# Turning norm rows and memory probabilities: eight 128x128 transposes a tile, or 32 products on the quarters of the array

## What is computed

```python
def rmsnorm(x, g):
    xf = x.astype(F32)
    y = xf * lax.rsqrt(jnp.mean(xf * xf, axis=-1, keepdims=True) + EPS)
    return (y * g.astype(F32)).astype(x.dtype)

# hybrid_layer, behind the mixer (gated DeltaNet, short conv, stick-breaking attention)
x = x + jnp.concatenate([y_a, y_b, y_c], axis=-1) @ w_mix_out

h = rmsnorm(x, norm_mem_g)                                        # "norm2" in the kernel
qm = rmsnorm((h @ w_mq).reshape(B, T, MEM_HEADS, MEM_DH), mq_norm_g)
s = jnp.einsum('bthd,bnhd->bhtn', qm, mem_k) * (MEM_DH ** -0.5)
p = jax.nn.softmax(s, axis=-1)                                    # 4 heads, 256 memory tokens
om = jnp.einsum('bhtn,bnhd->bthd', p, mem_v).reshape(B, T, MEM_W)
x = x + om @ w_mo

h = rmsnorm(x, norm_ffn_g)                                        # "norm3" in the kernel
gt, ffn_buf_new = causal_dwconv(h @ w_gate, ffn_buf, ffn_conv_w)
x = x + (jax.nn.silu(gt) * (h @ w_up)) @ w_down
```

## Time and profile before

| | |
|---|---|
| median of 3 runs | 947.84 us |
| profiled execution, time | 947.93 us |
| profiled execution, span | 946.2 us |
| TensorE busy | 934.1 us, 99% |
| DVE busy | 648.3 us, 69% |
| ACT busy | 451.9 us, 48% |
| POOL busy | 170.1 us, 18% |

### The profile page before, as it was taken

How to read it: one execution, slowest core, us unless ns; L and a number is a source line. 1 busy time by engine, 2 the same in 40 slices (tenths; PEclk the granted TensorE clock), 3 DMA queues, 4 the chain that set the end, 5 groups by cost and what they waited for, 6 DMA issues and landing times.

```text
span 946.2 us, 16664 instructions
## 1 busy us (share of the span) xinstructions
PE 934.1 (99%) x6807; PEld 847.1 (90%) x6807; DVE 648.3 (69%) x1083; ACT 451.9 (48%) x836; POOL 170.1 (18%) x198
## 2 busy tenths in 40 slices
PE   8999999999999999999999999999999999999998
PEld 7899888998889877899889999999999999888886
DVE  7627888777775556551666999999999999435321
ACT  6634444648565344464655445444444446333310
POOL 0071101103654331000002042222222220000000
PEclk9999999999999999999999999999999999999999
DMA  8624152121104084143903322222222224312221
GB/s 302 225 87 145 56 169 90 48 94 46 45 5 134 2 278 166 61 150 150 317 35 116 132 90 90 89 90 90 76 74 77 87 89 147 152 59 97 76 91 55
DMA packets 73819, 103.69 MB, mean 110 GB/s; under 512 B 2576, under 2 KB 53904, under 8 KB 73360
## 3 DMA queue, kind: packets, MB, share of 16 engines
q1 hardware_dynamic: 73744, 102.63, 32.0%
HBM read 92.27 MB, written 10.35 MB: 108 GB/s over the span
## 4 chain that ended last, share of the span: by engine, by line
PE 90%; DVE 4%; ACT 2%; issue 1%; POOL 1%; DMA 1%; SPq 0%; ACTq 0%; DVEq 0%; POOLq 0%
PE bank L1202 8%; PE bank L1204 8%; PE bank L1203 8%; PE bank L533 7%; PE bank L535 7%; PE bank L534 7%; PE bank L495 6%; PE bank L497 5%; PE bank L496 5%; PE bank L463 3%; PE bank L559 2%; PE bank L561 2%; PE bank L560 2%; PE bank L482 1%; PE bank L481 1%; PE bank L483 1%
## 5 line engine op out<-in xcount | busy, mean ns | idle before, releaser
L2150 DVE TENSOR_TENSOR wlo<-wraw,whi 128x2048 fp32r<-128x2048 f32 (+1 forms) x56 | 126.1, 2253 | 103.1 <-ACT whi L1599 93.8
L1599 ACT ACTIVATE whi<-wraw 128x2048 fp32r<-128x2048 f32 (+1 forms) x58 | 109.3, 1885 | 102.7 <-PE bank L535 72.9
L495 PE MATMUL bank<-hhi,whi 128*128 128x320 f32 x352 | 116.4, 331 | 0.6 <-issue 0.6
L497 PE MATMUL bank<-hhi,wlo 128*128 128x320 f32 x352 | 108.7, 309 | 0.0
L496 PE MATMUL bank<-hlo,whi 128*128 128x320 f32 x352 | 108.7, 309 | 0.0
L495 PEld LDWEIGHTS bank<-hhi,whi 128*128 128x128 f32 x352 | 66.2, 188 | 5.0 <-issue 3.6
L496 PEld LDWEIGHTS bank<-hlo,whi 128*128 128x128 f32 x352 | 66.2, 188 | 3.0 <-issue 2.4
L497 PEld LDWEIGHTS bank<-hhi,wlo 128*128 128x128 f32 x352 | 66.1, 188 | 0.0
L533 PE MATMUL bank<-whi,hhi 128*128 128x512 f32 x150 | 58.4, 389 | 0.0
L534 PE MATMUL bank<-wlo,hhi 128*128 128x512 f32 x150 | 58.4, 389 | 0.0
L535 PE MATMUL bank<-whi,hlo 128*128 128x512 f32 x150 | 58.3, 389 | 0.0
(11 more groups left out here) (489 smaller groups left out, 2701.9 us busy)
## 6 DMA issues: line engine op xcount, KB each, us to landing
wraw<-in_w_in SPq DMA_DIRECT2D x13, 1024.0 KB, 5.3
wraw<-in_w_gate SPq DMA_DIRECT2D x11, 1024.0 KB, 5.1
wraw<-in_w_up SPq DMA_DIRECT2D x11, 1024.0 KB, 5.1
wraw<-in_w_down SPq DMA_DIRECT2D x10, 1024.0 KB, 5.0
kTs<-in_cache_sb_k SPq DMA_DIRECT2D x8, 512.0 KB, 4.4
vraw<-in_cache_sb_v SPq DMA_DIRECT2D x8, 512.0 KB, 5.0
wraw<-in_w_mix_out SPq DMA_DIRECT2D x4, 1024.0 KB, 6.1
kmT<-in_cache_mem_k SPq DMA_DIRECT2D x8, 512.0 KB, 6.0
```

The lines of the kernel that those rows point to most:

```text
L495: T.matmul(o, wh[:, k, cs], hhi[:, k, hs], start=(k == 0), stop=False)
L497: ins = T.matmul(o, wl[:, k, cs], hhi[:, k, hs], start=False, stop=(k == KD - 1))
L1599: V(wv(whi, i), wv(wraw, i), ACT.Copy).then_inc(s["w_hi_ready"], 1)
L2150: V.tensor_tensor(wv(wlo, i), wv(wraw, i), wv(whi, i).bitcast(F32), ALU.subtract)\
```

## The change

`turn_rows` and, for the prompt's four tiles, `mem_probs` call a new helper, `turn_quarters`. For each 128x128 block of the source it issues four products of 64x64: row half g of the block (64 tokens) and column half c (64 features) is the stationary operand, the matching quarter of the unit matrix is the moving one. The product with g and c writes partitions of half c, in the bank of g. So a bank now holds all eight blocks for one half of the tile's tokens, where it held four blocks for all of its tokens. Both banks are taken ahead of the first product and both are marked full behind the last ones. The readers follow: hi_part and lo_part, and the copies of probT, take 8 pieces of 64 tokens instead of 4 of 128. The queries' first half of the tokens now asks for tiles 0, 1 and one half of tile 2. The samples' probabilities are turned as before, by eight 128x128 transposes.

```diff
--- before.py
+++ after.py
@@ -279,6 +279,9 @@
         def quad(b):
             return bank[b][:, :].rearrange("p (a b) -> p a b", a=4)
 
+        def eighths(b):
+            return bank[b][:, :].rearrange("p (a b) -> p a b", a=8)
+
         def conv_s(t):
             return t[:, PAD + SEQ:PAD + SEQ + DEC_BATCH * (PAD + DEC_SEQ)].rearrange("p (b t) -> p b t", b=DEC_BATCH)
 
@@ -568,15 +571,25 @@
                         else:
                             ends[i] = ("bank", (name, half, NT - 1))
 
+            def turn_quarters(outs, srcs):
+
+                for j, src in enumerate(srcs):
+                    last = []
+                    for g in range(2):
+                        for c in range(2):
+                            ins = T.matmul(bank[use[outs[g]][0]][half64(c), BLOCK * j:BLOCK * j + BLOCK],
+                                           src[half64(g), half64(c)], ident[half64(g), half64(g)], start=True, stop=True)
+                        last.append(ins)
+                for ins, key in zip(last, outs):
+                    done(ins, key)
+
             def turn_rows(kind, n, src, ready):
 
                 pe.wait_ge(s["xn_ready"], ready)
-                for g in range(2):
-                    b = take((kind, n, g))
-                    for j in range(4):
-                        ins = T.transpose(bank[b][:, j * P:(j + 1) * P], src[:, (4 * g + j) * P:(4 * g + j + 1) * P],
-                                          ident[:, :])
-                    done(ins, (kind, n, g))
+                outs = [(kind, n, g) for g in range(2)]
+                for key in outs:
+                    take(key)
+                turn_quarters(outs, [src[:, k * P:(k + 1) * P] for k in range(KD)])
 
             def scores(n):
                 kind, x, i = SB_ITEMS[n]
@@ -1035,10 +1048,10 @@
             memory_rows("mk", B_MK, 0, mk_banks)
             memory_rows("mk", B_MK, 1, mk_banks,
                         behind=lambda kk: turn_rows("norm2", PT, xn2[PT % 2], NT) if kk == 0 else None)
-            for h, tiles in ((0, (0, 1, 2)), (1, (3, PT))):
-                for n in tiles:
-                    for g in range(2):
-                        evacuated(pe, ("norm2", n, g))
+            turned = [(n, g) for n in range(NT) for g in range(2)]
+            for h in range(2):
+                for n, g in turned[NT * h:NT * h + NT]:
+                    evacuated(pe, ("norm2", n, g))
                 across_half(("mq", 0), B_MQ[0], h)
             across(("mq", 1), B_MQ[1], hhi, hlo, cs=(0,))
             for t in range(2):
@@ -1087,13 +1100,19 @@
 
             def mem_probs(i):
                 pe.wait_ge(s["prob_ready"], i + 1)
+                outs = [("pT", i, g) for g in range(2)]
+                if i < PT:
+                    for key in outs:
+                        take(key)
+                    turn_quarters(outs, [probs[i % 2][:, h, nb * P:(nb + 1) * P] for h in range(HEADS) for nb in range(2)])
+                    return
                 for g in range(2):
-                    b = take(("pT", i, g))
+                    b = take(outs[g])
                     for j in range(4):
                         h, nb = 2 * g + j // 2, j % 2
                         ins = T.transpose(bank[b][:, j * P:(j + 1) * P], probs[i % 2][:, h, nb * P:(nb + 1) * P],
                                           ident[:, :])
-                    done(ins, ("pT", i, g))
+                    done(ins, outs[g])
 
             def mem_values(i):
                 if i == 0:
@@ -1609,7 +1628,7 @@
             def hi_part(kind, n, dst):
                 for g in range(2):
                     b = filled(e, (kind, n, g))
-                    V(dst[:, 4 * g:4 * g + 4], quad(b), ACT.Copy).then_inc(s["h_hi_ready"], 1)
+                    V(dst[:, :, half64(g)], eighths(b), ACT.Copy).then_inc(s["h_hi_ready"], 1)
 
             LN_EXP = "natural_log_exp_and_others"
             e.preload_act_table_set(LN_EXP)
@@ -2006,7 +2025,7 @@
                     filled(e, ("om", i - 2))
                 for g in range(2):
                     b = filled(e, ("pT", i, g))
-                    V(probT[i % 2][:, 2 * g:2 * g + 2, :, :].rearrange("p h n t -> p (h n t)"), bank[b][:, :], ACT.Copy)\
+                    V(probT[i % 2][:, :, :, half64(g)].rearrange("p h n t -> p (h n) t"), eighths(b), ACT.Copy)\
                         .then_inc(bank_free[b], 1)
 
             def om_part(i):
@@ -2157,7 +2176,7 @@
                     lo_part.count += 1
                     dve.wait_ge(s["h_hi_ready"], lo_part.count)
                     b, _ = use[(kind, n, g)]
-                    V.tensor_tensor(lo[:, 4 * g:4 * g + 4], quad(b), hi[:, 4 * g:4 * g + 4].bitcast(F32), ALU.subtract)\
+                    V.tensor_tensor(lo[:, :, half64(g)], eighths(b), hi[:, :, half64(g)].bitcast(F32), ALU.subtract)\
                         .then_inc(bank_free[b], 1)
             lo_part.count = 0
             def hidden(k):
```

## The result

The changed kernel takes 951.27 us (median of 6 runs, 950.74 to 952.13), the kernel before 948.0 us (6 runs, 947.35 to 948.23): a ratio of 1.0036, with a 95% interval of 1.0023 to 1.0049. That is 3.3 us slower, inside the forecast range and 0.3 us from the forecast 951.6. The profiled execution of the changed kernel took 950.74 us, with a span of 949.0.

The account below looks back on a forecast made before the run. TensorE, busy 934.1 of 946.2 us, was taken to bound the kernel. Terms 1.26 + 0.50 + 1.91 = +3.67 us on 947.93 gave 951.6 us, range 949.8 to 953.4.

Parts of the forecast that it names:

- What a quarter product costs: On TensorE, four 64x64 products need two rounds, 0.117 us, against 0.110 us for the one transpose they replace.
- in and out: Fixed price on TensorE of changing between whole array and quarters: 0.35 us for a run of 32 products.
- Norm rows ahead of the memory layer: Turns of tiles 0 and 1 together +0.46 us, tiles 2 and 4 +0.40 each: sum +1.26 us.
- covered by wlo: Tile 3's +0.40 us ahead of the memory layer is hidden by the 0.9 us wait for wlo behind it.
- Probabilities: Memory attention, four turns: 1.40 us more on TensorE, 0.90 absorbed by idle time (anything from 0 to 0.9), +0.50 left.
- the chain: Between 458.6 and 481.8 us the chain of waits runs from memv to omlo through DVE and ACT, not TensorE.
- Norm rows ahead of the FFN: Tile 0 +0.31 us, its way in already paid, tiles 1 to 4 +0.40 each, nothing absorbed: sum +1.91 us.
- The later release, copies in pieces of 64: Both banks released at the last product, first copy 0.45 us later, copies in 8 pieces instead of 4: cost nothing.
- B: Rival: switching array shapes costs less beside 512-column products; half the fixed part gives back some 1.7 us, 949.9; chance 0.10.
- C: Rival: later release of both banks makes readers wait, 0.5 us at two or three places, 952.8 to 953.5; chance 0.08.
- D: Rival: the two column halves on one row half go in turn, 0.94 us more a tile, about 963 us; chance 0.03.
- E: Rival: not slower, unit-matrix products need one record each, 0.059 us a group instead of 0.110, 946.5 us; chance 0.04.

Follow-up runs that it names:

- one group ahead of each turn: Kernel before, its 128x128 transposes kept, plus one extra group of four 64x64 products ahead of each turn that the change touches: 952.14 us, ratio 1.0046.
- diagonal order: Changed kernel with each block's four quarters issued as (0,0), (1,1), (0,1), (1,0), so no two successive products share a row half: 951.09 us, one execution.
- shifts of 96 and 176: Changed kernel with 96 or 176 more instructions (24 or 44 products of 32x32x4) at the start of TensorE's stream: 951.94 and 952.13 us, one execution each.
- row halves: Changed kernel's banks and copies, but each 128x128 block turned by two 64-row transposes, 16 one-record transposes a tile: 947.53 us, ratio 0.9997 to the kernel before.

## Why the prediction was right

**What a quarter product costs.** Right to the hundredth: 0.117 us a group (turning twice: 0.94 us for eight groups) and 0.35 us in and out (1.74 - 0.45 - 0.94). Both came from the chunk stage, which runs the same shapes; the second is the larger part of the loss, 0.35 of 0.40 us at a single tile, and it was shown apart by the one group ahead of each turn (0.30).

**Norm rows ahead of the memory layer.** +1.29 us against +1.26. Tile 3 added nothing, covered by wlo as forecast: 2.46 us from L561 to L1023 in both kernels.

**Probabilities.** The step that was mis-sized: +0.05 us instead of +0.50. TensorE's own share was right (0.41, 0.22, 0.39 and 0.39 us, 1.41 in four turns against 1.40), but 1.38 us were absorbed, not 0.90. The forecast took the idle time from the list of waits. That idle time counts from the modelled end of the product ahead, and a 512-column product is listed with 0.39 us while its slot is 0.23. In the kernel before, the wait for wlo, start to start:

```profile
475.04 0.39 PE L561 MATMUL bank<-whi,omlo 128*128 128x512 f32 x1
475.74 0.47 PE L559 MATMUL bank<-whi,omhi 128*128 128x512 f32 x1 [0.32 <-DVE wlo L2150]
476.05 0.39 PE L560 MATMUL bank<-wlo,omhi 128*128 128x512 f32 x1
```

From L561 to the second product behind are 1.01 us, two slots are 0.45: 0.56 lost, where 0.32 is listed. At the wait for omlo 1.92 us pass from the turn to L560, where 1.10 do without a wait, so 0.82 are lost and 0.58 listed. The sum, 1.38 us, is what a change could hide, and the four turns take just that: from turn 0 to turn 4 the probabilities need 28.45 us in the changed kernel and 28.48 before. In the kernel before this stage is paced by DVE and ACT, as the chain said. In the changed kernel it no longer is: TensorE has no wait left there, and from 458 to 484 us the chain of work that ended last runs through TensorE alone, turns included:

```profile
466.40 1.09 PE bank L580 x64
467.50 3.59 PE bank L1141 x64
```

So the cover is used up, and that it fits the four turns so closely is chance. The run with one group ahead of each turn, where a turn costs 0.43 us, confirms its size: of 1.7 us in the memory attention 0.33 come through. The forecast had bounded absorption by 0.9 from above, and that bound was wrong.

**Norm rows ahead of the FFN.** +2.15 us against +1.91, and 0.18 of it is the hole in tile 0's turn. With the diagonal order and with the shifts of 96 and 176, where this turn has no hole, the same part adds 1.91, 1.92 and 1.91 us: tile 0 0.21 to 0.22 instead of 0.31, tile 3, where 320-column products follow, 0.46 instead of 0.40, the others 0.39 to 0.42. So the sum was right to the hundredth, with two small errors in it that cancel.

**The later release, copies in pieces of 64.** Nothing. ACT's hi copy has a median of 592 ns (593 in the earlier trace rows). The first copy of probabilities 0 starts at 462.73, 1.2 us behind its turn's start instead of 0.6, and no product waits for it.

**The rivals.** B (cheaper switch beside 512 columns) fell: the fixed part is the same there. C fell: no new wait. D fell: the diagonal order changes nothing, and the records are 14.7 ns apart on average (four within 20 ns, the next four 58.3 behind). E fell: two records for each product. What is left is one error of the forecast, 0.45 us too much at the probabilities. The profiled sum, 3.45 us against 3.67, looks closer than it is, since it contains the hole; the two executions without holes behind the first turn, diagonal order and shift of 176, end 3.27 and 3.24 us late.

## What to carry to other kernels

Splitting a full-array operation into quarters is no gain by itself: half the columns only pays if the small product leaves no more records than the large one did (a 128x128 block took 0.110 us whole, 0.117 in quarters with two records each, 0.064 in row halves with one each), and every run of small products between large ones pays a switch (here 0.30 to 0.35 us for 4, 16, 32 or 64 products). So price one slot and one switch from a stretch of the trace that already has both, and count switches rather than products. And measure a wait from start to start against the slot without it; the listed idle time understates what a wait can absorb, here by 0.24 us each time.

## What the runs showed that was not expected

A dense run of small products (a load and a product every 14.7 ns on average) can break off for 0.2 to 1.6 us with no semaphore to wait for, always 1.25 to 1.59 us behind the end of a packet of code where the idle time is listed, and where that happens depends on how many instructions stand ahead in the stream: 48 more at the start of the program removed two holes worth 0.85 us from one kernel, 96 more put one of 1.15 us into another. The packets grow with TensorE's records: the kernel before has 54, the changed one with 784 records more 60, the one that turns every tile twice with another 896 has 67. The last two read, on their pages:

```profile
q8 instruction: 60, 0.98, 0.4%
```

```profile
q8 instruction: 67, 1.10, 0.5%
```

The same idle time also comes and goes between executions where the stream is the same: in the chunk stage it was 1.0 us in the profiled execution of the kernel before and 0.2 in that of the changed one, 0.9 with the quarters in diagonal order and none with row halves. The seven kernels here that were not shifted and start with the same stream as the kernel before reach the product ahead of the first turn between 384.57 and 385.52 us, the kernel before at 385.41. So a comparison of two kernels with short products carries up to about 1 us that belongs to neither. Behind the first turn the kernel before shows no such hole and the changed one only the 0.18 us in norm3's tile 0, within the 3.45 us of the table.
